# Router and token rows computed in token layout, first experts' rows by one-hot products

## The chip, the cores and the metric

The kernel runs on one core of a Trainium2 chip. The metric is the device time of one execution in microseconds; less is better. TensorE (PE), VectorE (DVE), ScalarE (ACT), GpSimd (POOL) and SyncE (SP, which issues most loads) run their own instruction streams and wait for each other on semaphores.

## What is computed

A first block (adaptive norm, a mixer of convolution, recurrence and gated linear attention, then a hierarchical mixture of experts), followed by a second model of two layers. All is float32; 512 tokens, width 1024. The change touches the entry of the mixture of experts:

```python
h = rms_norm(x, g_ffn) * (1.0 + sc2) + sh2          # sh2: a shift per channel
g_logits = hf @ w_rg + b_rg                          # 4 groups
e_all = einsum("bsd,gde->bsge", hf, w_re) + b_re     # 4 experts in each
# best group, its best two experts, weights comb; then for 16 experts
hid = silu(h @ w_gate) * (h @ w_up) * comb
y = y + hid @ w_down
```

## The kernel before

Activations lie as channels x tokens, `x` as 8 tiles of 128 channels x 512 tokens. A float32 product that must be exact is made of three products of split operands: ACT makes the high part (a copy to fp32r), DVE or POOL the low part (a subtraction), TensorE `mm3` (L1402) the three products. Weights of the first model come as chunks of 512 KB through `raw` (SP `stream_pair` L487; ACT `hi` L674; POOL `low` L603); the last two are tile 8 of the output projection and, as chunk C_RT, the router.

**Output projection and norm.** TensorE adds nine mixer tiles into 8 banks (`out_tile` L1571, each 8 x `mm3`); bank by bank DVE adds them to `x` (L2323). ACT squares `x` (`square` L687), TensorE sums the squares over channels with a matrix of ones (`stat` L1408), ACT makes the root (`inverse_root` L697), DVE scales (L2334), ACT adds the shift and makes `hf` and its high part `hh` (L861, L863), DVE the low part `hl` (L2329). TensorE transposes `hf` to token rows (L1609, L1622) and makes the logits as 20 x 512 by `mm3` (L1613), which ACT copies and TensorE turns to tokens x 20 (L1618).

**Routing.** DVE works out the routing in small steps (L2360 to L2414): the set of chosen experts, `R(9)`, goes to TensorE, which makes each token's rank in its expert (L1628). From the ranks DVE makes one-hot matrices `sel` (`select` L2416: slot = rank, four operations for a table's experts), and TensorE multiplies them with `combS` (`table` L1632), which gives for each expert's 128 slots the weight, the token's row number and the result's row number. DVE reads these out (`table` L2427). There are five tables, for experts 0; 1 to 3; 4 to 7; 8 to 11; 12 to 15.

**Rows.** ACT evacuates the transposed tokens (`h_tok`, L869), SP stores them as `h_rows` in memory (L545), POOL gathers each expert's 128 rows by index (`gather` L616), TensorE transposes them (`turn_rows` L1650) into two banks, ACT and DVE split them (`rows_hi` L878, `rows_lo` L2454: `gh`, `gl`).

**Experts.** Each has 12 chunks of weights, 512 KB: 4 gate, 4 up, 4 down. Chunks go through 12 raw buffers (three in `m_first`, six in `m_raw`, three in `hf`, once that is free) and 6 split buffers; SP loads them in order (`load_expert` L514, a chunk waits until the one 12 before it is lowered), ACT splits (`m_split` L849, waits for its split buffer to be used), DVE lowers (`m_low` L2401). TensorE runs `into` for gate and up (L1660), `turn_hid` (L1671), `down_rows` (L1680); ACT `silu` (L884), DVE `hidden` (L2462) and `hid_low` (L2470). The turn of expert E on TensorE (`expert` L1692) is gate and up of expert E+1, the turn of the rows of E+2, and down of E. Each engine's order is written out by hand, and each engine works strictly in that order: in front of the loop the tables are put between the first weight chunks, then `Fori(0, NE - 2)` runs the experts.

```python
            turn_rows(0)
            table(3)
            pe.wait_ge(gl_ready, 2)
            into(B_G, 0, 0)
            into(B_U, 4, 4)
            turn_rows(1)
            table(4)
            idle_work(0, 2)
            pe.wait_ge(tab_ready, len(TABLES))
            with pe.Fori(0, NE - 2) as E:
                expert(E, False)
```

In the projection stage before the mixer TensorE makes 22 column tiles by `proj` (L1417), the last four at L1460 to L1467; DVE then starts with the short convolution (L2200).

Of the kernel before, what the change touches and what calls it, by code (L numbers as in the profile page):

```python
# [45 lines left out]
TABLES = ((0, 1), (1, 4), (4, 8), (8, 12), (12, 16))  # L46
B_TAB = (4, 5)
# [60 lines left out]
ADDS = [sum(max(0, m - 1) for m in SUMMED[:n]) for n in range(3 * NL + 1)]  # L108
# [45 lines left out]
B_TOK = ((2, 3, 4, 5), (6, 7, 0, 2))  # L154
# [15 lines left out]
def columns(parts):  # L170
# [11 lines left out]
    ("b_i", NR), ("lam", NR), ("gla_b", 2), ("gla_g", GH), ("router_b", 20), ("eps", 1), ("one", 1), ("token", TT), ("y_row", TT), ("slot", 1)])  # L182
# [7 lines left out]
def build(nc, xT, cond, ada, wstream, gu_stream, vecs, lvecs, const, masks, lru_gates, gla_gate, moe_stream, na_bias, sw_bias, h_rows, y_rows, out):  # L190
    ctx = ExitStack()
    with ctx:
# [50 lines left out]
        def phase(parts):  # L243
# [23 lines left out]
        rlog, combS, comb_slot, h_idx, y_idx, ysb, hf, m_raw, m_hi, m_lo, m_first = phase([  # L267
# [3 lines left out]
            ("m_lo", [P, M_SLOTS, D], F32R), ("m_first", [P, 3, D], F32)])  # L271
# [7 lines left out]
        h_tok = m_mem[:, 2 * M_SLOTS * D:(2 * M_SLOTS + TT) * D].rearrange("p (t k) -> p t k", t=TT)  # L279
# [128 lines left out]
        def over_w(c):  # L408
# [42 lines left out]
        (ov_in, ov_used, ov_prod, ov_c_mm, ov_c, ov_row, ov_b, ov_mm, ov_silu, ov_hid, ov_down, ov_x) = (  # L451
            sem(n) for n in ("ov_in", "ov_used", "ov_prod", "ov_c_mm", "ov_c", "ov_row", "ov_b", "ov_mm", "ov_silu", "ov_hid", "ov_down", "ov_x"))
# [19 lines left out]
        def _(sp):  # L472
# [70 lines left out]
            for tt in range(TT):  # L543
                sp.wait_ge(tok_ready, TT + tt + 1)
                sp.dma_start(h_rows[tt * P:(tt + 1) * P, :], h_tok[:, tt, :]).then_inc(h_rows_out, 16)  # L545
            sp.wait_ge(h_ready, 2 * KD)
# [55 lines left out]
        def _(pool):  # L602
# [13 lines left out]
            def gather(E):  # L616

                if E > 0:
                    pool.wait_ge(rows_mm, E)
# [35 lines left out]
            for E in range(NE):  # L655
# [10 lines left out]
        def _(act):  # L666
# [197 lines left out]
            act.wait_ge(w_used, C_RT + 1)  # L864
# [5 lines left out]
            for n in range(3):  # L870
                m_split(n, n)
# [1245 lines left out]
        def _(dve):  # L2117
# [213 lines left out]
            for k in range(KD):  # L2331
# [4 lines left out]
                if k >= 1:  # L2336
                    low(k - 1)
# [793 lines left out]
```

## Time and profile before

| what | value |
|---|---|
| three runs, median (lowest to highest) | 2783.74 us (2782.13 to 2788.76) |
| the profiled execution, time | 2782.57 us |
| its span | 2780.7 us |
| mean granted clock of TensorE, share of full speed | 0.986 |
| TensorE busy, records | 2687.7 us, 15906 |
| DVE, ACT, POOL busy | 1986.5, 1456.6, 122.1 us |

Times in rows are microseconds from the span's start. A row of the engine views is start, duration, engine, line, operation, output<-inputs, shapes and a count; in brackets stands the idle time before it and what ended it. Consecutive instructions of one line are merged into one row, and its duration reaches to the end of the last, so that the step from one instruction to the next is read from the start of the following row.

### The profile page before, as it was taken

What the parts mean: (1) busy time and instruction counts of PE and PEld (TensorE: products, weight loads), DVE (VectorE), ACT (ScalarE), POOL (GpSimd) and SP (SyncE); (2) the same over time, 40 slices, a digit from 0 to 9 for tenths busy, and PEclk for the clock granted to TensorE, in tenths of its full rate; (3) what the DMA queues carried; (4) which work ended last, traced back from release to release, by engine and by line L of the source; (5) the groups of instructions that cost most, each with busy time, mean ns of one, the idle gap of its engine ahead of it and who ended that gap; (6) DMA issues with size and microseconds to landing.
All of it is one profiled execution on the core that took longest, in us unless ns stands there. A gap on an engine that the chain in (4) does not pass through costs nothing.

```text
span 2780.7 us, 45770 instructions
## 1 busy us (share of the span) xinstructions
PE 2687.7 (97%) x15906; PEld 2309.6 (83%) x15906; DVE 1986.5 (71%) x2871; ACT 1456.6 (52%) x2187; POOL 122.1 (4%) x72
## 2 busy tenths in 40 slices
PE   5999899998999989999999999999999999999999
PEld 3866678885999867788899987999877888899987
DVE  7854689996898566653699947899555753699954
ACT  3353478885555246753555525555336753455532
POOL 1432111100000000000000000000000000000000
PEclk9999799998999999999999999999999999999999
DMA  7731499993332331123233232332333113323222
GB/s 285 276 136 38 169 349 409 405 374 122 103 105 83 102 144 61 53 76 114 91 107 106 91 108 89 99 100 89 101 103 115 60 62 112 108 92 106 91 97 100
DMA packets 95245, 377.57 MB, mean 136 GB/s; under 512 B 10833, under 2 KB 11105, under 8 KB 92897
## 3 DMA queue, kind: packets, MB, share of 16 engines
q1 hardware_dynamic: 89072, 348.69, 35.7%
q0 software_dynamic: 4608, 16.78, 1.5%
q10 hardware_dynamic: 1456, 10.66, 1.0%
q8 instruction: 68, 1.11, 0.2%
q14 instruction: 41, 0.33, 0.0%
HBM read 363.50 MB, written 16.78 MB: 137 GB/s over the span
## 4 chain that ended last, share of the span: by engine, by line
PE 85%; DVE 6%; issue 5%; ACT 3%; DMA 0%; POOL 0%; SPq 0%; ACTq 0%; POOLq 0%; DVEq 0%
PE pb L1404 16%; PE pb L1406 15%; PE pb L1405 15%; PE pb L1789 10%; PE pb L1791 10%; PE pb L1790 10%; PE pb L1973 1%; PE pb L2005 1%; PE pb L1929 1%; PE pb L1478 1%; ACT SP L1286 1%; DVE hid L2689 1%; PE pb L1657 1%; PE pb L1982 1%; DVE SP L2841 0%
## 5 line engine op out<-in xcount | busy, mean ns | idle before, releaser
L1789 PE MATMUL pb<-bl,g_wh 128*128 128x256 f32 x2464 | 701.9, 285 | 9.7 <-DVE bl L2600 5.7
L1790 PE MATMUL pb<-bh,g_wl 128*128 128x256 f32 x2464 | 697.9, 283 | 0.0
L1791 PE MATMUL pb<-bh,g_wh 128*128 128x256 f32 x2464 | 697.8, 283 | 0.0
L1789 PEld LDWEIGHTS pb<-bl,g_wh 128*128 128x128 f32 x2464 | 473.4, 192 | 14.3 <-issue 8.2
L1790 PEld LDWEIGHTS pb<-bh,g_wl 128*128 128x128 f32 x2464 | 473.5, 192 | 1.6 <-issue 1.4
L1791 PEld LDWEIGHTS pb<-bh,g_wh 128*128 128x128 f32 x2464 | 473.6, 192 | 0.0
L2639 DVE TENSOR_TENSOR w_lo<-raw,w_hi 128x1024 fp32r<-128x1024 f32 x164 | 200.3, 1223 | 201.9 <-ACT w_hi L679 201.1
L1404 PE MATMUL pb<-hl,w_hi 128*128 128x512 f32 (+1 forms) x728 | 304.1, 418 | 20.5 <-DVE hl L2133 9.8
L679 ACT ACTIVATE w_hi<-raw 128x1024 fp32r<-128x1024 f32 x194 | 204.2, 1057 | 190.8 <-PE pb L1406 176.7
L1405 PE MATMUL pb<-hh,w_lo 128*128 128x512 f32 (+1 forms) x728 | 287.1, 394 | 0.0
L1406 PE MATMUL pb<-hh,w_hi 128*128 128x512 f32 (+1 forms) x728 | 286.9, 394 | 0.0
L1404 PE MATMUL pb<-fl,w_hi 128*128 (+1 forms) x576 | 225.0, 391 | 1.7 <-DVE w_lo L2645 1.4
L1404 PEld LDWEIGHTS pb<-hl,w_hi 128*128 128x128 f32 (+1 forms) x728 | 137.1, 188 | 67.2 <-issue 29.9
L1405 PE MATMUL pb<-bl,w_lo 128*128 128x512 f32 x448 | 174.3, 389 | 0.0
L1406 PE MATMUL pb<-bl,w_hi 128*128 128x512 f32 x448 | 174.3, 389 | 0.0
L1089 ACT ACTIVATE htmp<-pb 128x256 f32<-128x256 f32 x264 | 101.0, 384 | 139.7 <-PE pb L1791 139.7
L1405 PEld LDWEIGHTS pb<-hh,w_lo 128*128 128x128 f32 (+1 forms) x728 | 137.8, 189 | 31.5 <-issue 6.2
L1406 PEld LDWEIGHTS pb<-hh,w_hi 128*128 128x128 f32 (+1 forms) x728 | 137.5, 189 | 30.8 <-issue 0.7
L2509 DVE TENSOR_TENSOR g_wl<-g_own,g_wh 128x1024 fp32r<-128x1024 f32 x132 | 137.9, 1044 | 21.7 <-ACT g_wh L935 17.8
L1102 ACT ACTIVATE bl<-hid 128x512 fp32r x56 | 35.4, 632 | 217.4 <-PE pb L1406 217.4
L2694 DVE TENSOR_TENSOR fl<-hid,bl 128x512 f32 x56 | 38.8, 692 | 147.3 <-ACT bl L1102 147.3
L1404 PEld LDWEIGHTS pb<-fl,w_hi 128*128 128x128 f32 x576 | 108.1, 188 | 26.1 <-DVE w_lo L2645 3.3
(450 smaller groups left out, 5355.6 us busy)
## 6 DMA issues: line engine op xcount, KB each, us to landing
raw<-in_wstream SPq DMA_DIRECT2D x220, 512.0 KB, 3.3
m_raw<-in_moe_stream SPq DMA_DIRECT2D x96, 512.0 KB, 6.1
g_own<-in_gu_stream SPq DMA_DIRECT2D x44, 768.0 KB, 4.2
raw<-in_gu_stream SPq DMA_DIRECT2D x44, 768.0 KB, 4.2
m_first<-in_moe_stream SPq DMA_DIRECT2D x48, 512.0 KB, 6.0
hf<-in_moe_stream SPq DMA_DIRECT2D x48, 512.0 KB, 5.2
ada_ring<-in_ada SPq DMA_DIRECT2D x8, 2048.0 KB, 8.1
g_own<-in_gu_stream SPq DMA_DIRECT2D x44, 256.0 KB, 3.1
```

The costliest lines, as they stand in the source:

```text
L679: act.activation(w_hi[s][:], raw[s][:], ACT.Copy).then_inc(w_hid, 1)
L1089: act.activation(split_of(n), pb[bank][:, 0:HALF], ACT.Copy, scale=scale).then_inc(g_cp, 1)
L1102: act.activation(f_hi_of(k, s), row(hid, k), ACT.Copy).then_inc(f_hi, 1)
L1404: pe.matmul(o, lh, rl, start=first, stop=False)
L1405: pe.matmul(o, ll, rh, start=False, stop=False)
L1406: return pe.matmul(o, lh, rh, start=False, stop=last)
L1789: pe.matmul(o, lh, rl, start=first and k == 0, stop=False, skip_group_check=True)
L1790: pe.matmul(o, ll, rh, start=False, stop=False, skip_group_check=True)
L1791: m = pe.matmul(o, lh, rh, start=False, stop=k == 3, skip_group_check=True)
L2509: dve.tensor_tensor(g_wl[:, w, :, :], frm, g_wh[:, w, :, :].bitcast(F32), ALU.subtract).then_inc(g_lo, 1)
L2639: dve.tensor_tensor(w_lo[s][:], raw[s][:], w_hi[s][:].bitcast(F32), ALU.subtract).then_inc(w_lod, 1)
L2694: dve.tensor_tensor(row(fl, k), row(hid, k), f_hi_of(k, s).bitcast(F32), ALU.subtract).then_inc(f_lo, 1)
```

## The change

- The router and the token rows take `x * gain` before the norm's factor is known. ACT makes this product per tile of `x`, beside the square. The factor, one per token, is applied later in token layout: on the logits by DVE, on the rows by ACT's evacuation.
- Sums of squares: DVE adds the eight squares, TensorE sums channels with four products that give one column each. ACT takes the root of 4 columns.
- The shift: for the logits, router weights times shift, summed by TensorE once in the projection stage; for the rows, a rank-one product of the token's root and the shift's row into the same banks, before evacuation. Transposes become products with the identity, so that the rank-one product can be added. In every bank only the first product has the clearing flag.
- Logits come as tokens x 20, in float32, from 4 products a tile, put between the products of the last output tiles. The router's weights come with the vectors; chunk C_RT stays in the stream, with zeros.
- The rows of experts 0 and 1 are made by TensorE from `h_tok` and `sel` (`gather_rows`), no longer by POOL's gather. `h_tok` now is `hf`, so chunks 9 to 11 wait until both are made.
- Tables are cut as 0, 1; 2, 3; then fours. Tables 2 and 3 go into expert 0's turn, 4 behind it; expert 0 is taken out of the loop. The two filler products in front of it go.
- Small constants for later norms move on DVE from the router to the projection stage.

The diff, cut to what matters (comments name the engine's stream):

```diff
-TABLES = ((0, 1), (1, 4), (4, 8), (8, 12), (12, 16))
-B_TAB = (4, 5)
+TABLES = ((0, 2), (2, 4), (4, 8), (8, 12), (12, 16))
+B_TAB = (4, 5, 4, 0, 0)
...
-        h_tok = m_mem[:, 2 * M_SLOTS * D:(2 * M_SLOTS + TT) * D].rearrange("p (t k) -> p t k", t=TT)
+        h_tok = hf[:].rearrange("p (h t) c -> p t h c", h=2)
...
             # SP
-            sp.wait_ge(h_ready, 2 * KD)
+            sp.wait_ge(h_rows_out, 16 * TT)
+            sp.wait_ge(rows_mm, 2)
             for n in range(9, M_RAW):
                 load_expert(n, n, n + 4)
...
             # POOL
-            for E in range(NE):
+            for E in range(2, NE):
...
             # ACT
-            his(C_WOUT // 2 + 2, 2)
-            squares(1, lambda k: act.wait_ge(x_ready, k + 1))
-            norm_root(1)
+            for s in range(2):
+                hi(C_WOUT // 2 + 3, s)
+            hi(C_RT // 2, 0)
+            for k in range(KD):
+                act.wait_ge(x_ready, k + 1)
+                if k >= 4:
+                    act.wait_ge(sq_sum, max(1, k - 4))
+                act.activation(x_sq[k % 4], x[:, k, :], ACT.Square).then_inc(sq_ready, 1)
+                act.activation(hf[:, k, :], x[:, k, :], ACT.Copy, scale=gs[:, 1, k:k + 1]).then_inc(hf_ready, 1)
+            act.wait_ge(stat_mm, 2 * KD)
+            act.activation(ln_ms, pb[1][:, 0:TT], ACT.Ln, scale=1.0 / D, bias=V("eps")).then_inc(root_ready, 1)
+            act.wait_ge(root_ready, 2)
+            act.activation(root_tok, ln_ms, ACT.Exp, scale=0.5)
+            act.activation(rs_tok, ln_ms, ACT.Exp, scale=-0.5).then_inc(rs_ready, 1)
+            act.wait_ge(lg_tok, 2)
+            act.activation(stemp[:], pb[1][:], ACT.Copy).then_inc(hf_ready, 1)
+            hi(C_RT // 2, 1)
...
-            for k in range(KD):
-                act.wait_ge(h_tmp, 8 + k + 1)
-                act.activation(hf[:, k, :], htmp[:, k % 2, :], ACT.Identity, bias=modv[:, 32 + k:33 + k]).then_inc(hf_ready, 1)
-                act.wait_ge(hf_ready, k + 1)
-                act.activation(hh[:, k, :], hf[:, k, :], ACT.Copy).then_inc(h_hi, 1)
+            for tt in range(TT):
+                token_rows(0, tt)
             act.wait_ge(route, 1)
             act.activation(R(1)[:, :, 0:4], R(1)[:, :, 0:4], ACT.Exp).then_inc(route_exp, 1)
+            m_split(0, 0)
             act.wait_ge(route, 3)
             act.activation(R(6)[:, :, 0:1], R(6)[:, :, 0:1], ACT.Exp).then_inc(route_exp, 1)
-            for n in range(3, M_SLOTS):
-                m_split(n, n)
+            m_split(1, 1)
+            for tt in range(TT):
+                token_rows(1, tt)
+            m_split(2, 2)
...
             rows_hi(0)
-            for n in range(M_SLOTS, M_SLOTS + 4):
+            for n in range(3, M_SLOTS + 4):
                 m_split(n, n)
             silu(0, 4)
             for n in range(M_SLOTS + 4, M_SLOTS + 8):
                 m_split(n, n)
+            act.wait_ge(m_used, 8)
             rows_hi(1)
...
             # PE, projection stage, before the last two column tiles
+            pe.wait_ge(mod_ready, 3)
+            for k in range(KD):
+                pe.matmul(pb[3 + k // 4][64 * (k // 4):64 * (k // 4) + 1, k % 4 * P:(k % 4 + 1) * P], modv[:, 32 + k:33 + k], ident, start=True, stop=True)
+            for k in range(KD):
+                m = pe.matmul(pb[5][:, 0:20], ones, shifted_w[:, k, :], start=k == 0, stop=k == KD - 1)
+            m.then_inc(consts_or_ov_c_mm, 1)
...
+            def logits(k):
+                pe.wait_ge(hf_ready, k + 1)
+                for tt in range(TT):
+                    m = pe.matmul(pb[0][:, 20 * tt:20 * tt + 20], hf[:, k, tt * P:(tt + 1) * P], router_w[:, k, :],
+                                  start=k == 0 and tt == 0, stop=k == KD - 1, skip_group_check=True)
...
+            def turn_tokens(half, tiles):
+                for tt in tiles:
+                    for k in range(4):
+                        pe.matmul(pb[B_TOK[half][tt]][:, k * P:(k + 1) * P], hf[:, 4 * half + k, tt * P:(tt + 1) * P], ident,
+                                  start=k == 0, stop=False, skip_group_check=True)
+            def shift_tokens(half):
+                for tt in range(TT):
+                    row = slice(64 * half, 64 * half + 1)
+                    pe.matmul(pb[B_TOK[half][tt]][:], stemp[row, tt * P:(tt + 1) * P], shift_row[row, :],
+                              start=False, stop=True, skip_group_check=True).then_inc(turn_mm, 1)
...
+            mix_tile(NMIX - 2, range(KD - 2))
+            for m in range(KD):
+                if m >= KD - 2:
+                    ins = mix_tile(NMIX - 2, (m,))
...
+                ins = mix_tile(NMIX - 1, (m,))
...
+                if m >= 3:
+                    logits(m - 3)
+            logits(5)
+            turn_tokens(0, range(TT))
+            for k in range(6, KD):
+                logits(k)
+            pe.wait_ge(sq_sum, KD - 1)
+            for tt in range(TT):
+                m = pe.matmul(pb[1][:, tt:tt + 1], rs[:, tt * P:(tt + 1) * P], ones[:, 0:1], start=True, stop=True)
+            m.then_inc(stat_mm, KD)
+            turn_tokens(1, range(2))
+            pe.wait_ge(rs_ready, 2)
+            for tt in range(TT):
+                m = pe.matmul(pb[1][:, tt * P:(tt + 1) * P], root_tok[:, tt:tt + 1].broadcast_to([P, P]), ident, start=True, stop=True)
+            m.then_inc(lg_tok, 1)
+            pe.wait_ge(hf_ready, KD + 1)
+            shift_tokens(0)
             chunk(C_RT // 2, 1)
+            pe.sem_inc(w_used, 1)
+            pe.wait_ge(tok_ready, 2)
+            turn_tokens(1, range(2, TT))
...
             m.then_inc(rank_mm, 1)
+            shift_tokens(1)
...
+            def gather_rows(E):
+                pe.wait_ge(sel_ready, E + 1)
+                for k in range(KD):
+                    for tt in range(TT):
+                        m = pe.matmul(pb[B_T[k // 4]][:, k % 4 * P:(k % 4 + 1) * P], h_tok[:, tt, k // 4, k % 4 * P:(k % 4 + 1) * P],
+                                      sel[0][:, tt, E, :].bitcast(F32), start=tt == 0, stop=tt == TT - 1)
+                    if E == 0 and k == 3:
+                        m.then_inc(turn_mm, 1)
+                m.then_inc(rows_mm, 1)
...
+            def two_tables():
+                for g in (2, 3):
+                    table(g)
+                pe.wait_ge(tab_ready, 3)
-            turn_rows(0)
-            table(3)
-            pe.wait_ge(gl_ready, 2)
+            pe.wait_ge(tok_ready, 2 * TT)
+            gather_rows(0)
             into(B_G, 0, 0)
+            gather_rows(1)
+            table(0)
+            counts()
             into(B_U, 4, 4)
-            turn_rows(1)
+            table(1)
+            expert(0, False, two_tables)
+            pe.wait_ge(tab_ready, 4)
             table(4)
-            idle_work(0, 2)
-            pe.wait_ge(tab_ready, len(TABLES))
-            with pe.Fori(0, NE - 2) as E:
+            with pe.Fori(1, NE - 2) as E:
...
             # DVE, order from the ranks on
+            pick(lambda tt: sel[0][:, tt, 0:1], 0, 1)
+            m_low(0, 0)
+            m_low(1, 1)
...
+            rows_lo(0)
+            m_low(2, 2)
+            m_low(3, 3)
...
+            pick(lambda tt: sel[0][:, tt, 1:2], 1, 2)
+            for n in range(4, 8):
+                m_low(n, n)
             table(0)
...
+            select(1)
+            for n in range(8, 12):
                 m_low(n, n)
             hidden(0, 8)
             rows_lo(1)
+            table(1)
+            for n in range(12, M_SLOTS + 8):
+                m_low(n, n)
+            expert(0, False, {1: lambda: select(2), 4: lambda: select(3), 10: lambda: select(4)},
+                   lambda: [table(g) for g in (2, 3)])
             table(4)
-            with dve.Fori(0, NE - 2) as E:
+            with dve.Fori(1, NE - 2) as E:
```

## Rows read from the trace of the kernel before

**Rows 1.** Page: TensorE's busy time, the chain by engine.
```profile
PE 2687.7 (97%) x15906; PEld 2309.6 (83%) x15906; DVE 1986.5 (71%) x2871; ACT 1456.6 (52%) x2187; POOL 122.1 (4%) x72
...
PE 85%; DVE 6%; issue 5%; ACT 3%; DMA 0%; POOL 0%; SPq 0%; ACTq 0%; POOLq 0%; DVEq 0%
```

**Rows 2.** Stretches: us, PE, PEld, DVE, ACT, POOL busy, clock, DMA, GB/s.
```profile
126.00:167.70 41.70, 41.70 (x185) 34.04 (x183) 9.91 (x12) 18.89 (x20) 26.52 (x13) 1.00 0.34 116
...
290.88:301.60 10.72, 7.59 (x17) 2.38 (x16) 2.37 (x4) 5.92 (x10) 0.00 (x0) 0.95 0.42 148
...
325.40:339.40 14.00, 13.71 (x65) 13.63 (x65) 13.38 (x32) 1.09 (x2) 2.48 (x2) 0.50 0.53 170
339.40:353.20 13.80, 13.80 (x50) 10.98 (x51) 11.22 (x16) 8.53 (x9) 0.00 (x0) 0.80 0.95 315
353.20:359.85 6.65, 4.50 (x29) 3.19 (x28) 6.18 (x11) 2.35 (x4) 3.44 (x1) 1.00 0.79 267
359.85:378.07 18.22, 18.22 (x85) 14.82 (x85) 14.36 (x14) 13.50 (x15) 0.94 (x1) 1.00 0.84 291
378.07:396.20 18.13, 18.13 (x86) 14.76 (x85) 16.73 (x17) 15.31 (x18) 2.54 (x2) 1.00 0.99 385
```

**Rows 3.** TensorE in order of time: start, us, instruction, count, [idle before, releaser].
```profile
167.67 1.98 PE L1472 MATMUL pb<-z,glaw 16*128 16x512 f32 x4
169.58 7.14 PE L1478 MATMUL pb<-u_pad,diag 128*128 128x512 f32 x16
...
290.88 7.59 PE L1411 MATMUL pb<-sq,con 128*128 128x512 f32 x16
301.61 1.09 PE L1609 MATMUL pb<-con,hf 128*128 128x128 f32 x4 [3.13 <-ACT hf L861]
...
319.53 1.89 PE L1628 MATMUL pb<-rlog,con 128*128 128x64 f32 x8 [4.25 <-DVE rlog L2377]
...
326.22 1.87 PE L1645 MATMUL pb<-rlog,con 128*128 128x16 f32 x8
327.93 2.72 PE L1638 MATMUL pb<-combS,sel 128*128 128x4 f32 x12
...
353.95 1.93 PE L1638 MATMUL pb<-combS,sel 128*128 128x4 f32 x16
...
359.85 0.50 PE L1404 MATMUL pb<-m_lo,gh 128*128 128x512 f32 x1 [2.15 <-DVE y_idx L2437]
```

**Rows 4.** VectorE in order of time, same columns.
```profile
167.78 0.55 DVE L2202 TENSOR_SCALAR mt<-z,vec 128x512 f32<-128x512 f32 x1 [31.81 <-PE pb L1406]
...
286.40 5.43 DVE L2323 SCALAR_TENSOR_TENSOR x<-pb,modv,x 128x512 f32<-128x512 f32 x8 [32.72 <-PE pb L1406]
...
314.67 0.24 DVE L2360 TENSOR_TENSOR rlog<-pb,vec 128x80 f32<-128x80 f32 x1 [0.95 <-PE pb L1618]
...
319.25 0.23 DVE L2377 TENSOR_TENSOR rlog<-rlog 128x64 f32<-128x64 f32 x1
...
350.06 2.50 DVE L2422 TENSOR_TENSOR sel<-con,rlog 128x512 fp32r<-128x512 f32 x4
352.47 2.36 DVE L2405 TENSOR_TENSOR m_lo<-hf,m_hi 128x1024 fp32r<-128x1024 f32 x2
...
357.67 1.28 DVE L2458 TENSOR_TENSOR gl<-pb,gh 128x512 fp32r<-128x512 f32 x2
```

**Rows 5.** ScalarE in order of time, same columns.
```profile
292.00 0.63 ACT L690 ACTIVATE sq<-x 128x512 f32<-128x512 f32 x1 [3.52 <-PE pb L1411]
...
348.90 1.28 ACT L888 ACT_TABLE_LOAD   x1
...
354.49 1.07 ACT L882 ACTIVATE gh<-pb 128x512 fp32r<-128x512 f32 x2
```

**Rows 6.** GpSimd in order of time; then L518, the experts' loads, to landing.
```profile
286.83 2.41 POOL L606 TENSOR_TENSOR w_lo<-raw,w_hi 128x1024 fp32r<-128x1024 f32 x1 [3.12 <-ACT w_hi L679]
...
DMA to landing us min/median/max: 3.5/5.9/7.2
```

More of the change, by code:

```diff
@@ L919, in _ @@
                 m_split(n, n)
+            act.wait_ge(m_used, 8)
             rows_hi(1)
-            with act.Fori(0, NE - 2) as E:
+            expert(0, False)
+            with act.Fori(1, NE - 2) as E:
                 expert(E, False)
@@ L1690, in down_rows, with expert @@
                     m.then_inc(m_used, 1)
-            def expert(E, last):
+            def expert(E, last, tables=lambda: None):
                 n0 = N_EXP * E + M_AHEAD
@@ L1699, in expert @@
                 into(B_U, n0 + 4, M_AHEAD + 4)
+                tables()
                 if not last:
@@ L2439, in _ @@
-            select(0)
-            select(1, range(2))
-            table(0)
-            select(1, range(2, TT))
-            dve.wait_ge(rank_mm, 2)
-            step(dve.tensor_reduce(small[:, 200:201], pb[1][:, TT * NE:(TT + 1) * NE], AX, ALU.max))
-            dve.tensor_copy(most[:], small[0:1, 200:201]).then_inc(most_ready, 1)
-            select(2)
-            table(1)
-            dve.wait_ge(h_rows_out, 16 * TT)
-            m_low(0, 0)
-            select(3)
-            m_low(1, 1)
@@ L2452, in _ @@
-            table(2)
-            m_low(2, 2)
             def rows_lo(E):
@@ L2474, in hid_low, with expert, lows @@
                                   hidTh[:].rearrange("p k t -> p (k t)").bitcast(F32), ALU.subtract).then_inc(hidT_lo, 1)
-            def expert(E, last):
+            def expert(E, last, before={}, tables=lambda: None):
                 n0 = N_EXP * E + M_AHEAD
-                for c in range(4):
-                    m_low(n0 + c + M_SLOTS, M_AHEAD + c + M_SLOTS)
+                def lows(first, end):
+                    for c in range(first, end):
+                        if c in before:
+                            before[c]()
+                        m_low(n0 + c + M_SLOTS, M_AHEAD + c + M_SLOTS)
+                lows(0, 4)
@@ L2491, in _ @@
             m_low(3, 3)
-            table(3)
-            for n in range(4, M_SLOTS + 4):
-                m_low(n, n)
-            select(4)
-            for n in range(M_SLOTS + 4, M_SLOTS + 8):
+            for g in range(NG):
+                ins = dve.scalar_tensor_tensor(combS[:, :, EG * g:EG * g + EG, 3], o2, float(T),
+                                               V("y_row", 0, TT).unsqueeze(2).broadcast_to([P, TT, EG]), ALU.mult, ALU.add)
+            step(ins)
+            step(dve.tensor_tensor(o1, o1, w1.broadcast_to([P, TT, 4]), ALU.mult))
@@ new lines, in _ @@
+            step(dve.tensor_tensor(o2, o2, psel.broadcast_to([P, TT, 4]), ALU.mult))
+            step(dve.tensor_tensor(o1, o1, o2, ALU.add))
+            dve.tensor_tensor(by_group(R(8)[:, :, 0:NE]), selx,
+                              o1.unsqueeze(2).broadcast_to([P, TT, 4, 4]), ALU.mult).then_inc(route, 1)
+            dve.wait_ge(route, 4)
+            step(dve.tensor_copy(combS[:, :, :, 0], R(8)[:, :, 0:NE]))
+            step(dve.tensor_tensor(combS[:, :, :, 1], R(8)[:, :, 0:NE], combS[:, :, :, 0].bitcast(F32), ALU.subtract))
@@ L2497, in _ @@
+            pick(lambda tt: sel[0][:, tt, 1:2], 1, 2)
+            for n in range(4, 8):
+                m_low(n, n)
+            table(0)
+            dve.wait_ge(rank_mm, 2)
+            step(dve.tensor_reduce(small[:, 200:201], pb[0][:, P:P + NE], AX, ALU.max))
+            dve.tensor_copy(most[:], small[0:1, 200:201]).then_inc(most_ready, 1)
+            select(1)
+            for n in range(8, 12):
                 m_low(n, n)
```

237 lines of the change are left out of this document (109 added, 128 removed).

## The prediction, made before the changed kernel was run

> **What bounds the kernel now.** I read the page first: TensorE is busy 97% of the span and holds 85% of the chain that ended last, so a change counts by the TensorE work and the TensorE waits that it adds or takes away [rows 1]. Then the table by stretch [rows 2], to see where TensorE isn't full or runs at the lower of its two clocks (0.50 is 1.2 GHz, 1.00 is 2.4 GHz). The work before the mixer is full at 1.00 (126 to 167.7). Between the output projection's end (290.88) and the steady expert loop lie the losses: 10.72 us with 7.59 busy, 14 us at 0.50, 13.8 us at 0.80, 6.65 us with 4.50 busy. From 359.85 on every expert takes 18.1 to 18.2 us at 1.00 with no TensorE idle, while DVE is busy 16.73 of 18.13. Third, TensorE in order of time [rows 3]: it idles 3.13 us for the first normed tile, 4.25 us for the routing, 2.15 us for the last table; the clock fell after the first two and not after the third. Fourth, DVE and ACT in order of time [rows 4, 5]: from 350 DVE works without a pause, and it begins `gl` for expert 1 only at 357.67, 4.5 us after the gate and up products of expert 0 are done.
>
> The whole change therefore lies in one question: when does expert 1's turn begin? It is now 378.07 [rows 2]. After that nothing differs but the loop's first index. I work in the times of the profiled execution (2782.57 us, 1.2 under the median) and carry the difference to the median.
>
> **Prices.** A float32 product is two records. 512 columns: 16 records in 7.14 us, 0.44 each, so 0.88 a product; with few rows it is no cheaper (4 records of 16 rows from 167.67 to 169.58, 0.48 each) [rows 3]. With 128 columns or fewer a record is bound by its 128x128 weights: 8 records in 1.71 us at the low clock (326.22 to 327.93), 0.21, hence 0.107 at the high one; the table's 16 records at the high clock take 1.93 with the last one's tail, 0.11 to 0.12 [rows 3]. I take 0.11 a record, 0.22 a product; the upper bound is 0.43 at the low clock. A chunk of expert weights is 1.4 us: 18.13 less 12 transposes, by twelve [rows 2].
>
> **Constants in the projection stage.** 8 shift rows and 8 products for the router's offset, 32 records: 3.5 us on TensorE in a stretch where it is full; DVE has idled 31.81 us there and starts only on TensorE's last projection [rows 2, 4]. So all later work moves by **+3.5**. The moved small DVE operations, the row copies and the offset's add lie in that idle time: nothing. I add the 3.5 at the end; times below are without it.
>
> **Router and norm.** Removed: 8 sums of squares (290.88 to 298.3), the root and norm chain, 28+4 transposes, 24 products, all the time to 314.67, when routing starts on DVE [rows 3, 4]. Added: the last two projection tiles are interleaved, so the first bank ends 1.36 us earlier (286.40 becomes 285.05 on DVE) [rows 4]. ACT needs 0.63 for a square and 0.63 for the scaled copy [rows 5], 1.2 a tile. TensorE has 1.55 a tile (0.68 of projection, 0.87 for 8 logit records), so it is its own bound: logits 0 to 4 end at 284.06 + 6.82 + 4.4 + 0.3 of waits = 295.6. Logits 5 (0.9), 16 turns (3.5), logits 6 and 7 (1.75): 301.7. Four sums of one column (0.9): 302.6; three short ACT operations with their hand-overs, 1.0 by estimate (DVE's small steps take 0.2 each: 22 of them from 314.67 to 319.25 [rows 4]): 303.6, and routing starts on DVE at 303.7, **11 us earlier**. Its chain keeps its length (314.67 to 319.48) plus one operation [rows 4]: `route` at 308.9.
>
> TensorE meanwhile: 8 turns to 304.4, root spread (8 records) 305.3, ACT's copy 306.1, four rank-one shifts (3.5) 309.6. It then waits for chunk C_RT: that is still loaded, split and lowered, though its weights are zero. ACT splits it after its copy (1.06, to 307.4), POOL takes 2.41 [rows 6]: 310.0. 8 turns 311.8, rank products 312.7, four shifts 316.2. ACT's last evacuation: 316.9.
>
> **One-hot rows for experts 0 and 1.** They replace the store, the gather and the eight transposes for two experts. Each is 32 products, 64 records: 7.1 us against 0.9 for the transposes. Row 0 of experts: 316.9 to 324.0 (DVE: `sel` for expert 0 at 314.5, before it). Products of B_G 5.6: 329.6. `sel` for expert 1 is queued on DVE behind `gl` (325.3), two weight tiles (2.4), the table columns (nine small steps, 1.9) and takes four such steps itself, 0.9: 330.5, a wait of 1.0. Gather 1: 337.7. Table 0 and counts 1.8: 339.5. B_U 5.6: 345.1. Table 1 0.9: **346.0**. In the kernel before B_U ended at 353.16.
>
> **The wait in front of expert 0.** Chunks 9 to 11 go into `hf`, and the SP queue now holds them, with everything behind, until gather 1 is done (337.7). A load lands 3.5 to 7.2 us after issue [rows 6]; from an idle queue I take 3.7, and then 1.3 us a chunk (0.52 MB at some 400 GB/s, the steady stretch moved 385 [rows 2]): 9 lands at 341.4, 11 at 344.0, 13 at 346.6. ACT splits 9, loads its table (1.28 [rows 5]), does the silu and the splits of 10 to 13 at 1.0 each, and only then evacuates expert 1's rows (1.07 for two): 349.7. DVE: `gl` half by half, 350.4. TensorE waits **4.4 us**. Before it waited 2.15 with two filler products ahead.
>
> Idle gaps of 3.13 and 4.25 us were each followed by 0.50, one of 2.15 was not [rows 2, 3]; so the clock falls here. From 339.4 to 353.2 the mean is 0.80, that is 5.5 us of dense products at 0.50 before it came back [rows 2], which costs 2.7. The Trainium skill ("TensorE: Matmul & The Clock Gate", "HAM oscillation") says the same against this change: idle waits between bursts send the array back to half rate, and it must earn the full one again. By that rule the sum is +5.5, without any fall +5.0. The trace agrees with the fall.
>
> **Expert 0.** It now also carries tables 2, 3 (32 records, 3.55) and 4 (1.8). More important, DVE carries three more selects (four operations in 2.4 us), three tables (two small steps, 0.45 each) and two more weight tiles between 350.4 and the end: about 28 us of work, at 1.18 a weight tile [rows 4]. Step by step from 350.4: chunks 12 to 17 with select 2, 10.7; low half of the hidden rows 11.4; select 3, 13.8; chunks 18 to 21, 18.6; hidden 19.3; table 2, 19.7. TensorE is through B_U at 14.5 and the two tables at 18.1 and must wait for DVE to read table 2, whose bank the down products need: 19.8. Turn 20.7, down products 26.3. DVE: `gl` of expert 2 at 22.6, chunks 22 and 23 at 25.4, select 4 at 27.8. Table 4 waits for it: 27.9 to 29.7. So expert 0 takes **29.7 us instead of 18.2** [rows 2].
>
> **Sum.** 350.4 + 29.7 + 3.5 = 383.6 against 378.07: **+5.5 us**. The front gains 9.4 (359.85 to 350.4), expert 0 gives back 11.5, the constants cost 3.5. 2783.7 + 5.5 = 2789. A measurement of this kernel tells about 0.3%, 8.3 us, from no change: so my forecast is no difference that counts.
>
> **Rival A, the waits vanish.** TensorE's bare work from 285.43 to expert 1's turn: last tile 5.5, logits 7.0, turns 7.0, sums and spread 1.8, shifts 7.0, rank 0.9, gathers 14.2, counts 0.9, eight weight chunks 11.2, tables 7.1, expert 0 18.2: 80.8, to 366.2, with 3.5 to 369.7: **-8.4 us, 2775**. This is the floor. For it: six weight slots let DVE lag some microseconds. Against: 13 us of my waits would have to go, and DVE had only 1.4 us to spare in 18.1. Halfway (-2) is the likelier form. Chance 0.2.
>
> **Rival B, the low clock in the gathers (the slower side).** If TensorE idles as long as 3.13 us anywhere between 299 and 317 (it decides at the root's round trip through ACT and at C_RT's low part on POOL), the turns, shifts and gather 0 run at 0.50. From 325.4 to 339.4 TensorE was busy 13.71 of 14 and stayed at 0.50 [rows 2], so short products need not bring it back. Price: 17.7 us of work from 310 on doubled, +23 in all, **2807**; if it comes back after 5.5 us, +8, 2792. Against: my longest wait there is 0.8 us. Chance 0.1.
>
> **Rival C, chunks 9 to 13 land late.** With eleven loads issued at once the median landing (5.9 [rows 6]) instead of 3.7 may hold for chunk 9; silu and the rows of expert 1 are queued behind its split on ACT. Price 2.2 to 3.5: +8 to +9, **2792**. Chance 0.15.
>
> **Numbers.** My forecast has 0.55, spread 2785 to 2793. Range 2778 to 2800: it leaves out the floor of A and the full form of B. Faster by over 0.3% is only the floor: 0.06. Slower: B, most of C, a tenth of mine: 0.27. Same: 0.67.
>
> **What would show it.** In the changed profile: 32 short records near 157 and the mixer 3.5 us later; routing on DVE near 307; gathers of 64 records in 7.1 us each at clock 1.00; a TensorE idle of about 4 us released by `gl` before expert 0, with a fall of the clock; in expert 0 a wait for a table (DVE) of 1 to 2 us; expert 1's first weight products 5 us later than before. I am wrong if the gathers run at another price per record, if the constants are hidden, or if DVE isn't what expert 0 waits for.

## The result and the profile after

The changed kernel takes **2823.59 us** (median of 4 runs, 2822.49 to 2830.12) beside 2786.25 of the kernel before (2782.13 to 2789.48): ratio **1.0142, 95% interval [1.0126, 1.0158]**. It is slower by 37 to 40 us where 5.5 were forecast. The profiled execution has a span of 2820.7 us, 40.0 more than before. In run 1 below, one execution of six took 4460.65 us at a mean granted clock of 0.557; the comparison there leaves it out.

The table by stretch of the changed kernel, columns as in [rows 2]: the stretch up to the mixer's first products, the first shift up to gather 0, the two gathers, up to expert 0, and expert 0 up to expert 1's turn.

```profile
126.00:172.95 46.95, 46.95 (x220) 37.48 (x218) 17.04 (x21) 19.64 (x22) 28.12 (x13) 1.00 0.41 139
...
312.57:327.94 15.37, 14.60 (x40) 7.73 (x40) 8.49 (x26) 8.53 (x14) 2.34 (x1) 0.67 0.17 62
327.94:336.76 8.82, 8.82 (x64) 8.82 (x65) 0.69 (x1) 1.49 (x2) 0.00 (x0) 0.80 0.36 131
343.44:350.61 7.17, 7.17 (x65) 7.17 (x65) 4.49 (x4) 0.00 (x0) 0.00 (x0) 1.00 0.01 2
350.61:363.13 12.52, 8.42 (x51) 7.25 (x49) 8.88 (x19) 7.70 (x9) 0.00 (x0) 0.96 0.90 350
363.13:395.12 31.99, 27.93 (x133) 23.44 (x133) 26.83 (x42) 15.65 (x18) 3.75 (x3) 0.86 0.88 339
```

TensorE in order of time in the changed kernel, as in [rows 3]:

```profile
158.40 1.47 PE L1490 MATMUL pb<-con,modv 128*1 128x128 f32 x16
159.81 1.96 PE L1492 MATMUL pb<-small,con 128*128 128x20 f32 x16
172.95 1.98 PE L1503 MATMUL pb<-z,glaw 16*128 16x512 f32 x4
...
312.57 5.44 PE L1653 MATMUL pb<-shift_row,stemp 1*128 1x512 f32 x8 [0.69 <-ACT stemp L866]
...
383.02 1.97 PE L1730 MATMUL pb<-con,rows 128*128 128x128 f32 x8 [1.88 <-DVE y_idx L2503]
393.34 1.92 PE L1703 MATMUL pb<-combS,sel 128*128 128x4 f32 x16 [2.18 <-DVE sel L2482]
```

Three things are to be seen. The constants are there (32 records, 3.4 us), but the mixer starts 5.28 us late (172.95 against 167.67 [rows 3]), not 3.5. TensorE is busy from 313 to 337 at 0.67 and 0.80 of its clock. Expert 1's turn starts at 395.12 against 378.07 [rows 2], 17.05 late. Behind that, where the code is the same, 23 us more are lost. The page says where. Here are the kernel before, then the changed one:

```profile
L1405 PE MATMUL pb<-bl,w_lo 128*128 128x512 f32 x448 | 174.3, 389 | 0.0
...
L1405 PE MATMUL pb<-bh 128*128 128x512 f32 x64 | 24.9, 389 | 0.0
```

```profile
L1429 PE MATMUL pb<-bl,w_lo 128*128 128x512 f32 x448 | 177.0, 395 | 0.0
...
L1429 PE MATMUL pb<-bh 128*128 128x512 f32 x64 | 25.0, 390 | 0.0
```

(groups of instructions: busy us, mean ns of one.) Products of 512 columns that pair a streamed weight tile (`w_hi`, `w_lo`) with another tile last 395 ns instead of 389; from start to start it is 233 ns instead of 227 in the trace (232.6 on average instead of 227.3). Products that take both operands from tiles behind the vector tile keep their time: the 512-column ones of `bh` with `bh` (the second line of each pair) or with `fl`, and those of 256 columns. The change made the vector tile 640 bytes a partition longer, and every tile allocated behind it moved by that much; the weight tiles lie ahead of it and did not move. So the distance between the operands changed in the first kind of product and not in the second; the 256-column products therefore say nothing on what a distance costs. In the kernel before the experts' products were at 233 already.

### The profile page after: what moved, and what is told of

Its sections match the earlier page's. It is cut to its first block, busy times and chain, and to the rows that moved or that the text cites. A ratio compares the mean times of both kernels' runs of the same rounds, so it can differ in the third digit from the quotient of the medians.

```text
span 2820.7 us, 46172 instructions
## 1 busy us (share of the span) xinstructions
PE 2733.6 (97%) x16130; PEld 2336.4 (83%) x16130; DVE 1988.1 (70%) x2871; ACT 1451.3 (51%) x2180; POOL 119.4 (4%) x70
## 4 chain that ended last, share of the span: by engine, by line
PE 86%; DVE 6%; issue 4%; ACT 3%; DMA 0%; POOL 0%; SPq 0%; ACTq 0%; POOLq 0%; DVEq 0%
PE pb L1428 16%; PE pb L1430 15%; PE pb L1429 15%; PE pb L1873 10%; PE pb L1875 10%; PE pb L1874 10%; PE pb L2057 1%; PE pb L2089 1%; PE pb L2013 1%; PE pb L1509 1%; ACT SP L1310 1%; PE pb L1712 1%; PE pb L2066 0%; PE pb L1730 0%; DVE SP L2931 0%
## 5 line engine op out<-in xcount | busy, mean ns | idle before, releaser
L1428 PE MATMUL pb<-hl,w_hi 128*128 128x512 f32 x720 | 302.8, 421 | 19.3 <-DVE hl L2217 9.2
L1429 PE MATMUL pb<-hh,w_lo 128*128 128x512 f32 x720 | 286.3, 398 | 0.0
L1430 PE MATMUL pb<-hh,w_hi 128*128 128x512 f32 x720 | 286.2, 398 | 0.0
L1428 PEld LDWEIGHTS pb<-hl,w_hi 128*128 128x128 f32 x720 | 136.5, 190 | 67.8 <-issue 29.1
L1429 PEld LDWEIGHTS pb<-hh,w_lo 128*128 128x128 f32 x720 | 137.2, 191 | 34.0 <-issue 6.2
L1430 PEld LDWEIGHTS pb<-hh,w_hi 128*128 128x128 f32 x720 | 136.9, 190 | 32.1
```

What stands on the lines that cost most here:

```text
L1428: pe.matmul(o, lh, rl, start=first, stop=False)
L1429: pe.matmul(o, ll, rh, start=False, stop=False)
L1430: return pe.matmul(o, lh, rh, start=False, stop=last)
```

## Experiments

Theory P: what counts is the distance between the two operands of a product. Its rival is that other code or order slows TensorE.

Ratios are to the kernel before, timed beside each group of runs: its median was 2783.74 us beside runs 1 to 4, 2785.24 beside 5 to 8, 2783.93 beside 9 to 12, 2784.17 beside 13 and 14. Between groups, differences of medians are therefore uncertain by about 1.5 us, and the ratios are the better measure. The diffs are cut to what matters.

**1. before_plus640: the kernel before with 160 unused columns.**
```diff
-        vec = sb("vec", [P, NVEC])
+        vec = sb("vec", [P, NVEC + 160])
```


> The kernel before, with 160 unused columns (640 bytes a partition) behind the vector tile, so that every tile allocated after it lies where the changed kernel has it; nothing else differs. Theory P (placement): a float32r product of 512 columns whose weights lie in one of the two streamed weight tiles (allocated ahead of the vector tile, not moved) and whose moving operand lies behind it (moved), or the other way round, starts 233 ns after the one before instead of 227; products with both operands moved stay. Over all such products that is 17 to 20 us: 2786 becomes 2803 to 2806, and hl,w_hi / hh,w_lo / hh,w_hi are spaced 232 to 233 ns in the trace. Rival Q: the wider spacing in the changed kernel comes from its other code, order or DMAs; then this kernel is the kernel before, 2786 within 3 us, spaced 227.

Measured: 2804.2 us, ratio 1.0070 [1.0057, 1.0083]. The page has the 395 ns again, in code that is otherwise the kernel before:

```profile
L1405 PE MATMUL pb<-bl,w_lo 128*128 128x512 f32 x448 | 176.8, 395 | 0.0
...
L1405 PE MATMUL pb<-bh 128*128 128x512 f32 x64 | 24.9, 389 | 0.0
```

P holds. 160 columns that nobody reads cost 20 us. It is not quite the two operands of one product alone: the step to the next product is 232 to 233 ns where either of the two neighbours takes streamed weights. So 32 products of `fl` with `fl` that are followed by one with `w_hi` have a step of 232.5 ns, and the 352 pairs of neighbours without streamed weights one of 227.3. Which read of TensorE meets which is not shown.

**2. after_at_old_addresses: the changed kernel with every other tile back in place.** The router's weights get a tile at the end of the memory and a DMA of their own.


> The changed kernel, with the router's weights in a tile of their own at the end of the memory, loaded by their own DMA, so that every other tile lies where the kernel before has it. Theory P: the spacing of the products goes back to 227 ns, 17 to 20 us come back: 2804 to 2807, so the change itself costs 18 to 21 us, as the start of the expert loop (+18.7 at 1.4 of which placement) says. Rival Q: no change, 2823.

Measured: 2807.76 us, 1.0077 [1.0064, 1.0090]; spacing 227 ns. P holds; the change as such costs 24 us here and 18 in run 3.

**3. after_plus128: the changed kernel with 32 more columns behind the vector tile** (`NVEC + 32`).


> The changed kernel with 32 more unused columns behind the vector tile: all later tiles lie 768 bytes from where the kernel before has them instead of 640. It asks for the period of the placement. If what counts is the distance between the two operands modulo 256 bytes (or a divisor of it larger than 128), 768 is as good as 0 and the time is 2804 to 2807, spacing 227 ns. If it counts modulo 512 or more, it stays at 2823, 233 ns. Rival Q: 2823 too.

Measured: 2801.68 us, 1.0064 [1.0049, 1.0078], 22 us less than the changed kernel, spacing 227. So 0 and 768 bytes are good, 640 is bad: a multiple of 256 will do. Run 2 takes 6 us more than run 3, with intervals that overlap; in its profile the low clock behind the first shift lasted longer (0.50 from 313 to 336, in run 3 from 314 to 331). The cause stays open.

**4. before_experts_plus64: the kernel before with its experts aligned.**
```diff
-            ("h_idx", [P, NE], I32), ("y_idx", [P, NE], I32), ("ysb", [P, D], F32),
+            ("h_idx", [P, NE], I32), ("y_idx", [P, NE + 16], I32), ("ysb", [P, D], F32),
```


> The kernel before with 16 unused columns (64 bytes) among the tiles of the experts, ahead of the split weights. In the kernel before the distance from the split weights to the gathered rows and hidden rows is 192 modulo 256, and the products there start every 233 ns; now the distance is a multiple of 1024. Theory P: they start every 227 ns; 72 products an expert, 16 experts, 6 ns each is 7 us: 2779, unless VectorE, busy 16.7 of 18.1 us an expert, becomes the bound. Rival Q: no change, 2786.

Measured: **2778.46 us, 0.9982 [0.9973, 0.9991]**: 5.3 us faster than the kernel before. The products of the experts are now spaced 227 ns (233 before). One of their groups, in the kernel before and then here:

```profile
L1405 PE MATMUL pb<-m_hi,gl 128*128 128x512 f32 x256 | 102.1, 399 | 0.0
```

```profile
L1405 PE MATMUL pb<-m_hi,gl 128*128 128x512 f32 x256 | 100.5, 393 | 0.0
```

From here on run 3 is the base, so that only the change itself is left: its expert 1 starts at 395.32, 17.2 us later than before.

**5. k64_shift: 64 equal rows instead of one in the shift products.**
```diff
-                pe.matmul(pb[3 + k // 4][64 * (k // 4):64 * (k // 4) + 1, k % 4 * P:(k % 4 + 1) * P], modv[:, 32 + k:33 + k], ident, start=True, stop=True)
+                pe.matmul(pb[3 + k // 4][64 * (k // 4):64 * (k // 4) + 64, k % 4 * P:(k % 4 + 1) * P], modv[:, 32 + k:33 + k].broadcast_to([P, 64]), ident, start=True, stop=True)
...
-                    row = slice(64 * half, 64 * half + 1)
+                    row = slice(64 * half, 64 * half + 64)
```
and VectorE scales the copied rows by 1/64.


> Base is after_plus128 (2801.7). The eight shift products contract over 64 rows instead of one: the constant products put the shift into 64 equal rows each, scaled by 1/64, and the left side takes 64 equal rows. The number of records is the same. In the base the granted clock falls to 0.50 at 314.3, right behind the first four one-row products (3.7 us of them, no idle but 0.69 before), the second four take 7.19 us at 0.50, gather 0 takes 10.17 instead of the 7.2 of gather 1, and the wait in front of expert 0 ends at 361.70. Theory K: one-row products let the clock fall, as idle time does. Then it stays at 1.00 from 309 to 325, the second shift takes 3.6 us, turns and rank products 2.1 us less, gather 0 7.2: gather 0 ends 8 to 9 us earlier, expert 0 starts near 353, and the time is 2792 to 2794. Rival I: the 0.69 us of idle before them and the short products around are what let it fall: then the clock falls at the same place and the time stays at 2801 to 2802.

Measured: 2798.44 us, 1.0048 [1.0031, 1.0065], against 1.0064 of the base. TensorE in order of time, the base first, then this kernel:

```profile
309.55 3.69 PE L1653 MATMUL pb<-shift_row,stemp 1*128 1x512 f32 x8 [0.69 <-ACT stemp L866]
313.18 2.87 PE L1646 MATMUL pb<-con,hf 128*128 128x128 f32 x16
315.84 1.73 PE L1692 MATMUL pb<-rlog,con 128*128 128x64 f32 x8
317.49 7.19 PE L1653 MATMUL pb<-shift_row,stemp 1*128 1x512 f32 x8
325.46 10.17 PE L1712 MATMUL pb<-sel,hf 128*128 128x128 f32 x64 [0.78 <-ACT hf L884]
```

```profile
311.27 3.70 PE L1653 MATMUL pb<-shift_row,stemp 64*128 64x512 f32 x8 [0.69 <-ACT stemp L866]
314.90 2.05 PE L1646 MATMUL pb<-con,hf 128*128 128x128 f32 x16
316.79 0.96 PE L1692 MATMUL pb<-rlog,con 128*128 128x64 f32 x8
317.68 3.70 PE L1653 MATMUL pb<-shift_row,stemp 64*128 64x512 f32 x8
322.16 7.41 PE L1712 MATMUL pb<-sel,hf 128*128 128x128 f32 x64 [0.78 <-ACT hf L884]
```

From the first shift to the last record of gather 0 it is 25.8 us in the base and 18.1 here: theory K (one-row products let the clock fall) holds, at 7.7 us, for the mechanism. The total gained about half of that, 3.2 us by the medians and 4.5 by the ratios, with intervals that overlap; 2792 to 2794 was expected. In this execution the clock was low from 306 to 309 as well, right behind the products of 20 and 1 columns (they end at 306.04), which cost 1.6 (first shift at 311.27 against 309.55); and behind the wait for expert 0 it stayed low longer (expert 1's 24 gate records start within 7.79 us, in the base within 7.01). So the place of a fall and its length differ by some us between profiled executions whose code is the same at that place.

**6. hi_early: GpSimd's low part outside the routing.** ScalarE's `hi(C_RT // 2, 1)` stands ahead of its wait for the sums.


> Base is after_plus128 (2801.7). ScalarE splits the unused chunk behind the output projection before it waits for the sums of squares (it idles 5.9 us there) instead of behind its copy of the root, so GpSimd makes its low part near 302 to 304, outside the routing chain. In the base one VectorE operation of 128x16 takes 2.24 us at 310.66, for as long as that GpSimd operation (310.52 to 312.86); its neighbours take 0.17 to 0.18. Theory G: GpSimd holds VectorE up; now the routing chain is all 0.17 to 0.26 and ends 2.1 us earlier (311.8), ScalarE evacuates the first token rows 1 us earlier, and TensorE's turns wait less; of this up to 1 us can show before expert 0 (2800 to 2802), since TensorE has work until 317 anyway; in the chain of the rank products nothing waited for VectorE in the base. Rival: the 2.24 us is VectorE's own and stays, and the time too.

Measured: 2803.68 us, 1.0064 [1.0045, 1.0084], as the base. VectorE's operation at that place lasts 0.18 us (base: 2.24):

```profile
310.66 2.24 DVE L2437 TENSOR_TENSOR rlog<-rlog 128x16 f32<-128x16 f32 x1
```

```profile
311.76 0.18 DVE L2437 TENSOR_TENSOR rlog<-rlog 128x16 f32<-128x16 f32 x1
```

So GpSimd did hold it up (theory G), and it was off the path, as expected. The Trainium skill ("SBUF — State Buffer", "SBUF: two separate sides") says that the two engines share a pair of ports, held by one for a whole instruction; the trace agrees: 310.66 + 2.24 is 312.90, and GpSimd's operation ends at 312.86.

**7. silu_early: the silu of expert 0 ahead of the split of chunk 9.**


> Base is after_plus128 (2801.7). ScalarE does the silu of expert 0 (its gate products are done at 341) before it waits for chunk 9 of the weights, which lands at 353.1. In the base table load and silu stand behind that split, from 354.17 to 356.06, and expert 1's rows (gh at 359.74, gl to 361.65) are what TensorE waits 4.05 us for. Theory S: the 1.9 us leave the chain; splits 10 to 13 follow at once if their loads have landed, gl ends at 359.5 to 360, the wait is 2 to 2.6 us instead of 4.05, and the total falls by 1.5 to 2: 2799.5 to 2800.5. Rival L: chunks 10 to 13 land about when they are split, so nothing is gained: 4 us and 2801.7. If the clock does not fall any more behind the shorter wait, 1.5 more.

Measured: 2808.42 us, 1.0081 [1.0062, 1.0101]; the wait is 3.98 us instead of 4.05. Rival L holds: ScalarE waits 0.2 to 0.6 us for the landing of each of chunks 10 to 13. What the 6.7 us above the base are (4.7 by the ratios, whose intervals overlap) is not settled: its profiled span of 2801.3 is only 1.1 over the base's, and there the clock fell once more, behind the sums (0.50 from 308 to 311).

**8. three_and_aligned: the edits of runs 5, 6 and 7 on run 3, and the experts aligned as in run 4.**


> All three edits on after_plus128, and the 64 bytes ahead of the experts' split weights (run before_experts_plus64). If the effects add: 2801.7 less 8.5 (64-row shift), less 0 to 1, less 1.5 to 2, less 5 to 7 (spacing 227 ns in the experts) is 2783 to 2786: the gain of the front and its price in expert 0 cancel, and the kernel before with its experts aligned (2778.5) stays ahead. If one-row products are not what the clock falls for: 2791 to 2795.

Measured: 2790.37 us, 1.0016 [1.0007, 1.0026], 4 us above the range expected. In its profile the front is clean (1.00 from 304 to 351), and still expert 1 starts at 389.3: the front's gain is lost in three waits (5.10, 2.48 and 2.25 us), each with about 7 us at 0.50 that begin in it or right behind it. Run 8 is the base of the next runs.

**9. loads_ahead: loads that need not wait for gather 1 go first.**
```diff
+            for n in range(M_RAW, M_RAW + 7):
+                load_expert(n, n - M_RAW, n + 4)
             sp.wait_ge(rows_mm, 2)
             for n in range(9, M_RAW):
...
```


> Base is three_and_aligned (2790.4, profiled 2788.3). In the base the loads of chunks 9 to 11 wait for gather 1 (the token rows lie in their slots), and chunks 12 and on stand behind them in SP's queue, while the DMA engines idle from 328 to 343; from 344 on they are full, one chunk lands every 1.3 us, and ScalarE copies expert 1's rows only behind the splits of chunks 9 to 13 (13 at 352.52), so TensorE waits 5.10 us. Now chunks 12 to 18 are loaded ahead of 9 to 11, into slots that are free. Theory L: this wait is made of landings; chunk 11 lands near 349, splits 12 and 13 follow at once, gh near 351, gl 353.0 and the wait is 2.5 to 3 us instead of 5.1; if the clock does not fall at it, TensorE saves another 2 to 3. Total -2 to -5: 2785 to 2788. Rival: VectorE or ScalarE set the wait; then it stays at 5 us and 2790.

Measured: 2788.88 us, 1.0013 [1.0003, 1.0022]. The wait went from 5.10 to 2.78, as theory L (the wait is made of landings) says; the next wait, for table 2, grew from 2.48 to 3.24. The total gained 1.5 by the medians and 0.8 by the ratios, which is no difference that the runs show; 2785 to 2788 was expected.

**10. tables_free: a bank of its own for table 2, the last select earlier.** `B_TAB = (4, 5, 1, 0, 0)`; TensorE's wait for `tab_ready` 3 ahead of expert 2's rows goes, and one for the silu, which reads that bank, comes ahead of the tables; `select(4)` stands behind tables 2 and 3 on VectorE.


> Base is three_and_aligned (2790.4, profiled 2788.3). In expert 0 TensorE waits 2.48 us (VectorE must read table 2 out of a bank that the down products write) and 2.25 us (table 4 waits for its select, which stands behind two weight tiles on VectorE); each wait is followed by 4 to 5 us at a granted clock of 0.50. Now table 2 has a bank of its own (that of the gate products) and the last select comes before expert 2's rows, where VectorE idles 2.2 us. Theory D: the steps of my prediction for expert 0 hold (VectorE sets both waits), the waits go, and with them the falls of the clock: 4.7 us of waits and 2 to 5 us of clock, 2781 to 2784. Rival: what follows is late anyway (rows of expert 2, hidden rows), the waits reappear one step on, and the clock still falls: 2787 to 2790.

Measured: **2782.85 us**, 0.9994 [0.9983, 1.0004], 7.5 less than run 8 (6.1 by the ratios). Both waits are gone. TensorE in run 8, then here:

```profile
375.33 1.97 PE L1730 MATMUL pb<-con,rows 128*128 128x128 f32 x8 [2.48 <-DVE y_idx L2503]
386.70 2.70 PE L1703 MATMUL pb<-combS,sel 128*128 128x4 f32 x16 [2.25 <-DVE sel L2482]
```

```profile
373.79 1.09 PE L1730 MATMUL pb<-con,rows 128*128 128x128 f32 x8
381.78 1.84 PE L1703 MATMUL pb<-combS,sel 128*128 128x4 f32 x16
```

From the start of expert 0 to that of expert 1 it is 33.8 us in run 8 and 27.0 here. The clock still falls behind the tables, at 375.6, without any wait, but for 3 us instead of 7.

**11. both_ahead: the edits of runs 9 and 10.**


> The edits of loads_ahead and tables_free together, on three_and_aligned. If theories L and D both hold, the start of expert 1's turn comes from 389.3 to about 377, and the time is 2776 to 2779, that is 0.2 to 0.4% under the kernel before and level with it when its experts are aligned (2778.5). If the weight tiles on VectorE (1.18 us each, with three more selects) bound expert 0, 2781 to 2785.

Measured: 2782.00 us, 0.9991 [0.9982, 1.0001]; expert 1 starts at 379.77, not 377. The weight tiles don't bound it: no TensorE wait is left in expert 0. The clock is low from 353 to 356, at a wait of 2.93 us for expert 1's rows, and from 370 to 373, behind the tables. The total is not to be told from run 10 or from the kernel before.

**12. both_one_row: the same with one-row shifts.**


> As both_ahead, but with the shift products over one row as in the changed kernel. Theory K: the clock falls at them (it did in all five profiled kernels that have them, near 312 to 315, and in neither of the two with 64 rows), and 7 to 9 us of narrow products and gather run at 0.50: both_ahead plus 5 to 8 us. Rival: with 64 rows the fall only moves elsewhere; difference under 2 us.

Measured: 2790.17 us, 1.0020 [1.0010, 1.0030]: **8.2 us** more than run 11. From the first shift to the end of gather 0, in the table by stretch of this kernel, then of run 11:

```profile
312.24:331.11 18.87, 18.09 (x41) 9.56 (x41) 6.42 (x26) 7.65 (x13) 0.00 (x0) 0.54 0.18 67
331.11:339.75 8.64, 8.64 (x65) 8.64 (x65) 0.69 (x1) 1.49 (x2) 0.00 (x0) 0.82 0.59 206
```

```profile
310.66:321.55 10.89, 10.11 (x41) 5.59 (x41) 6.26 (x25) 7.64 (x13) 0.00 (x0) 1.00 0.12 46
321.55:328.71 7.16, 7.16 (x64) 7.16 (x65) 0.86 (x2) 1.49 (x2) 0.00 (x0) 1.00 0.61 225
```

The rows differ by 9.5 us. In each of the six profiled kernels with one-row shifts the clock fell at or right behind them, in none of the seven with 64 rows.

**13. rows_sooner: expert 1's rows ahead of the splits of chunks 12 and 13 on ScalarE.**


> Base is both_ahead (2782.0, profiled 2779.1). There TensorE waits 2.93 us in front of expert 0, and ScalarE copies expert 1's rows (gh, 351.81) only behind five splits; the products of expert 1 that come first need only chunks 8 to 11. Now the copy stands ahead of the splits of chunks 12 and 13. Theory L (the wait is the landing of chunks 9 to 11 behind gather 1 and the splits in front of the copy): gh starts at 350.0 instead of 351.81, gl ends 1.8 us earlier, the wait is 1.1 to 1.3 us. If the clock falls for the idle time, a shorter one saves up to 2 more: 2778 to 2780.5. Rival: the fall comes from the narrow table products in front of the wait (24 records of 4 and 16 columns in 1.8 and 0.8 us), then only 1.8 is saved.

Measured: 2780.61 us, 0.9986 [0.9976, 0.9996]. The wait was 2.73 us, not 1.2: ScalarE's copy does come right behind chunk 11, but chunk 11 itself was split only at 350.82, after its landing, and VectorE's low part and hidden rows stand between (until 353.72). So the wait is the landing of chunks 9 to 11, whose slots gather 1 holds; the splits behind them were hardly any of it.

**14. rows_sooner_filler: two products of no use in that wait** (`idle_work(B_H, 2)`, as the kernel before had; their result is not used).


> As rows_sooner, with two products of 512 columns into an unused bank (0.88 us each) in that wait, as the kernel before had (L1638 region, from 355.73). Their result is not used. Theory I (idle time lets the clock fall): expert 0 starts at 1.00 and takes 2 to 2.7 us less up to its hidden rows; they cost up to 0.6 beyond the wait: 2776 to 2779. Rival: it falls anyway, at the tables, and the fillers cost 0.5: 2779 to 2781.

Measured: **2779.50 us, 0.9983 [0.9974, 0.9992]**. The wait and expert 0 up to its hidden rows, run 13, then run 14:

```profile
352.30:355.06 2.76, 0.03 (x2) 0.01 (x1) 2.76 (x7) 2.44 (x4) 0.00 (x0) 1.00 0.86 272
355.06:362.60 7.54, 7.54 (x29) 6.05 (x29) 6.35 (x12) 3.28 (x4) 1.25 (x1) 0.77 0.94 337
```

```profile
351.43:354.12 2.69, 1.96 (x6) 0.65 (x6) 2.69 (x6) 2.38 (x4) 0.00 (x0) 1.00 1.00 286
354.12:360.06 5.94, 5.94 (x29) 4.92 (x29) 5.73 (x11) 3.29 (x4) 1.25 (x1) 1.00 0.91 332
```

The stretch behind the wait is 1.6 us shorter at a full clock, and the fall at 372 is gone with it. Theory I (idle time lets the clock fall) holds in the profile (span 3.6 us less). The medians differ by 1.1, inside their scatter, and 2779.5 lies above the 2776 to 2779 of theory I, where its rival's range begins: the total does not decide.

## Why the prediction was wrong

The mechanism that bore the forecast, a gain in front and a price in expert 0, is there, but the gain shows only where the clock is kept: expert 0 starts at 353.76 in run 11 against 359.85 before [rows 3], and at 361.70 in run 3. Three steps failed.

- **"After that nothing differs but the loop's first index."** This is the largest error, about 20 us of the 34 between the forecast and the profiled span (40.0 against 5.5). The diff adds 160 columns to a tile allocated ahead of most others, and I read that as data alone. Runs 1, 2 and 3 show it from both sides: 20 us come with the columns in the kernel before, 16 (run 2) to 22 (run 3) go from the changed one. No rival had it.
- **The clock in the front** (rival B: "Against: my longest wait there is 0.8 us"). The waits were as forecast, 0.69 and 0.78, and the rival's mechanism, an idle of 3 us, was wrong too: the clock fell while TensorE was busy with one-row products. In run 3, where the placement costs nothing, the first shift starts at 309.55 (forecast 306.1 + 3.5 = 309.6) and gather 0 ends at 335.39 instead of 327.5: 7.9 us. My price of a product "with few rows" came from a clock of 1.00 and held there (3.69 us for eight records); what such products do to the clock no row of before showed. Runs 5 and 12 size it at 7.7 to 9.5 us in the trace, run 12 at 8.2 in the median.
- **Expert 0 in 29.7 us.** 33.6 in run 3 (361.70 to 395.32). The waits were the ones named: 4.05 for `gl` (forecast 4.4), 2.74 for the tables (1.7), 2.18 for the last select (1.6). So 1.6 of the 3.9 us are longer waits for VectorE; the rest, by subtraction, is the low clock, which I had charged once and which came three times (0.50 from 362 to 366, from 379 to 386 and from 393 to 400). The second fall came within half a microsecond of the wait's start at 378.6, so it may as well belong to the narrow table products ahead of it; runs 10, 11 and 13 have such a fall with no wait.

So, in run 3's times, 17.2 us are the forecast's 5.5, 7.8 of clock in front and 3.9 in expert 0; the 2.3 that its span loses behind are the third low stretch, which reaches 4 us into expert 1. Right were the constants (3.4 us for 3.5; the mixer starts 3.0 us late in run 3, though 4.6 in run 2 and 1.0 in run 4, which has no constants, so this start varies by more than a microsecond between executions), gather 1 (7.17 for 7.1), the price of a record at 1.00, routing on VectorE (306.84 in run 3, forecast 307.2), the queue on SP, and what expert 0 waits for. The late landings of rival C did occur as a cause of that wait (run 7), within the 4.4 us given for it. Idle time did bear on the clock: behind the 2.73 us wait of run 13 it was 0.77, with that wait filled (run 14) 1.00. The Trainium skill ("TensorE: Matmul & The Clock Gate", "HAM oscillation") says that idle waits between bursts of work throttle the array again; these two traces agree.

## What to carry to other kernels

Before costing a diff, list the tiles whose address it moves: one trace of the kernel before with unused columns of the same size prices that alone. Here such a pad, put where it brings the experts' operands to the same residue modulo 256 bytes, was worth as much (2778.5, ratio 0.9982) as the whole change with all its repairs and that pad among them (2779.5, 0.9983). And price a short stall or a narrow product by the clock behind it: the two waits inside expert 0 of run 8 are 4.7 us by themselves, and without them (run 10) it was 6.8 shorter.

## What the runs showed of the hardware

- In these kernels a product of 512 columns of split operands starts every 227 ns when weights and moving operand lie a multiple of 256 bytes apart in a partition and every 232 to 233 when they do not (128 and 192 modulo 256 were seen; runs 1 to 4). No run changed the distance for 256-column products. The Trainium skill ("SBUF — State Buffer", "SBUF: two separate sides") says that among the engines only the port pair shared by VectorE and GpSimd causes contention and that TensorE never waits on anyone. Runs 1 and 4 show a cost for TensorE by addresses alone; whether that is a wait in the page's sense or something inside TensorE is not shown.
- During or right behind eight one-row records of 512 columns on a busy TensorE the granted clock fell to 0.50 (1.2 GHz) in six kernels of six (one profiled execution each), for 6 to over 20 us; the same records with 64 rows in none of seven.
- Products of 20 and 1 columns, without idle time, were followed by 0.50 in some executions (runs 5, 7 and 14) and not in others of nearly the same code; so were table products of 4 columns (runs 10, 11 and 13, not run 14).
